# Half of two output projections taken forward, three weight loads issued before a gather, and one pair's weight slots refilled in halves

## The chip, the core and the metric

The kernel runs on one core of a Trainium2 chip. The metric is the time of the program on the device in microseconds (us). Five engines run their own instruction streams and meet only at semaphores: PE (TensorE, matrix products and transposes), DVE (VectorE), ACT (ScalarE), POOL (GpSimd) and SP (SyncE, which here only issues DMA transfers, in the order of its program). Weights come from the chip's main memory through 16 DMA engines that all queues of the core share.

## What is computed

One inference step of a one-layer hybrid encoder, in float32: 528 prompt rows (16 learned rows and 512) and 32 rows of a running stream, 1024 channels each. Only the parts near the change:

```
h = rmsnorm(x); proj = h @ w_in
a_out = silu(layernorm(causal_dwconv(glu(...))))            # 512 channels
b_out = head_rmsnorm(stick_breaking(q, k, v))               # 512 channels
x = x + concatenate([a_out, b_out]) @ w_out                 # (1024, 1024)
h2 = rmsnorm(x, g_ffn)
# routing: top-1 of 4 groups, then top-2 of 8 experts in it, weights p
for e in range(32):
    gu = h2 @ w_e_in[e]                                     # (1024, 512)
    out += gates[:, e] * ((silu(gu[:, :256]) * gu[:, 256:]) @ w_e_out[e])   # (256, 1024)
x = x + out; y = rmsnorm(x, g_final)
```

Every expert's weights are read: 2 MiB of w_e_in and 1 MiB of w_e_out each, 96 MiB in all.

## The kernel before

The rows are held in five chunks: four of 128 rows (chunks 0 to 3) and chunk 4 with 64 (16 prompt rows, 16 empty ones, 32 stream rows). The order of work on each engine is written out by hand.

**Output projection.** `project(c, ks, ns)` multiplies chunk c's mixed activations `mixt` with the eight row blocks k of `wout`. Blocks 4 to 7 belong to attention, 0 to 3 to the convolution; `LATE` is the order (4, 5, 6, 7, 0, 1, 2, 3). A product of 128 rows, one k and one half n of 512 columns is two matmul records in the trace. For chunks 0, 1 and 2 the attention half is done before the convolution's activations are ready, and `LATE[4:]` follows. Chunks 3 and 4 are projected whole, with all eight blocks. For chunk 4 the two halves n use the two column halves of the array. The results stand in PSUM banks `OUT_BANK` = (4, 2, 6, 2, 6), each with its neighbour.

**Around it**, per chunk: DVE's `residual(c)` adds the product to x (semaphore `x2_ready`), `normed_h2(c)` makes the normalized row block h2 (with a sum of squares on ACT and a root on POOL), SP stores it to `h2_dram`, PE's `turn_h2(c)` transposes it into banks 0 and 1, ACT copies it, PE's `logits(c)` multiplies it with the router's weights, and DVE's `choose(c)` and `place_at(c)` pick the two experts of each row and the row's place within the expert's tile; `positions(c)` on PE counts the rows ahead. PE's order is: project 0, project 1, turn 0, half of project 2, logits 0, turn 1, other half of project 2, logits 1, half of project 3, turn 2, positions 0, other half of project 3, positions 1, logits 2, project 4, turn 3, positions 2, logits 3, turn 4, logits 4, and then the tables. DVE's order is: residual and h2 of 0, 1, 2, then choose 0, choose 1, place 0, residual 3, place 1, h2 3, choose 2, residual 4, h2 4, place 2, choose 3, places, choose 4, places.

**Experts.** They run in 16 pairs. For pair g POOL gathers the rows of both experts (64 each) with an indirect DMA, PE transposes them (`turn`), multiplies with w_e_in (`gate_up`), ACT and DVE form the activation, PE transposes and multiplies with w_e_out (`down`), ACT scales, and POOL scatters to `y_dram`. w_e_in goes through seven slots `wi` (expert e in slot e % 7), w_e_out through seven slots `wo`. A slot's refill waits on SP for `gu_done` (gate_up of the pair) or `y_done` (down of the pair). Slot `wi[6]` lies over blocks 4 to 7 of `wout`; slot 4 over `mixt`; slot 5, in two pieces `wi5`, and `wo[4]` lie over the h2 buffers, the router's weights, its logits and the transposed h2.

Everything that SP issues stands in one program order, which around the change is: experts' loads 2, 3, 0, 1; stores of h2 0 to 3; expert 4; store of h2 4; expert 6; then, after the logits, the routing's subtraction (`gsub_ready`) and the landing of gather 0 (`gathered[0]`), slot 5, `wo[4]`; after `ent_ready` `wo[6]`; and then the refills pair by pair, experts 7 and 8 first.

Of the kernel before, what the change touches and what calls it, by code (L numbers as in the profile page):

```python
# [11 lines left out]
ALU = mybir.AluOpType  # L12
# [53 lines left out]
def build(nc, x_prompt, x_sample, cache_k, cache_v, cache_conv, meta, g_mix, w_in, conv_w, conv_b,  # L66
          ln_g, ln_b, g_sb, w_out, g_ffn, w_rg, b_rg, w_re, b_re, w_ei, w_eo, g_fin,
          y_p, y_s, nk_p, nv_p, ncv_p, nk_s, nv_s, ncv_s):
    with ExitStack() as ctx:
# [3 lines left out]
        def sem(name):  # L73
            return ctx.enter_context(nc.semaphore(name))
# [104 lines left out]
        wi5 = [(slice(0, 6), lowf[:, 9216:12288].rearrange("p (k n) -> p k n", k=6)),  # L179
               (slice(6, KD), lowf[:, 6144:7168].rearrange("p (k n) -> p k n", k=2))]  # L180

        def wi_at(e, k):

            if e % WI_SLOTS == 5:
                return wi5[k // 6][1][:, k % 6, :]
            return wi[e % WI_SLOTS][:, k, :]
# [102 lines left out]
        wi_end_loaded = wv_loaded[0:2]  # L289

# [156 lines left out]
        MEAN_BANK, LN_BANK = 2, 0  # L447
# [36 lines left out]
        def _(sp):  # L484
# [124 lines left out]
            sp.wait_ge(h2_stored[1], 16 * 2)  # L609
            sp.wait_ge(gsub_ready, 3)  # L610
# [264 lines left out]
        def _(pe):  # L875
# [268 lines left out]

            def project(c, ks, ns=(0, 1)):
                w = ROWS[c]

                def ready(k):
                    if k < NI and c == 0:
                        pe.wait_ge(mixa_ready, k + 1)  # L1150
                    elif k == NI:
                        pe.wait_ge(mixb_ready, mixed(c))

                if w < P:
                    for k in ks:
                        for n in ns:
                            mm = pe.matmul(ps[w * n:w * n + w, OUT_BANK[c] + n, :], mixt[:, k, P * c:P * c + w],
                                           wout[:, k, 512 * n:512 * n + 512], start=k == LATE[0], stop=k == LATE[-1],
                                           skip_group_check=True)
                    mm.then_inc(res_done, 1)  # L1160
                    return
                for n in ns:
                    for k in ks:
                        if n == ns[0]:
                            ready(k)
                        mm = pe.matmul(ps[0:w, OUT_BANK[c] + n, :], mixt[:, k, P * c:P * c + w],  # L1166
                                       wout[:, k, 512 * n:512 * n + 512], start=k == LATE[0], stop=k == LATE[-1],
                                       skip_group_check=True)
                if ks[-1] == LATE[-1] and ns[-1] == 1:
                    mm.then_inc(res_done, 1)  # L1170
# [117 lines left out]
            project(0, LATE[4:])  # L1288
            project(1, LATE[4:])
# [14 lines left out]
            project(4, LATE)  # L1304
# [27 lines left out]
            def gate_up(g):  # L1332
                for e in (2 * g, 2 * g + 1):
                    pe.wait_ge(wi_loaded[e % WI_SLOTS], (e // WI_SLOTS * 16 + 16) * (2 if e % WI_SLOTS == 5 else 1))
# [5 lines left out]
                for k in range(KD):  # L1340
# [399 lines left out]
        def _(dve):  # L1740
# [305 lines left out]
            def residual(c):  # L2046
# [3 lines left out]
                if w == P:  # L2050
                    dve.tensor_tensor(x[0:w, c, :].rearrange("p (a n) -> p a n", a=2), x[0:w, c, :].rearrange("p (a n) -> p a n", a=2),
                                      ps[0:w, OUT_BANK[c]:OUT_BANK[c] + 2, :], ALU.add).then_inc(x2_ready, 1)
                else:
                    for n in range(2):
# [3 lines left out]
            def normed_h2(c):  # L2058
# [25 lines left out]
                dve.tensor_scalar(h, h, stat[0:w, 32 + c:33 + c], None, ALU.mult).then_inc(h2_ready, 1)  # L2084

# [55 lines left out]
            normed_h2(0)  # L2141
            residual(1)
# [197 lines left out]
```

## Time and profile before

| | us |
|---|---|
| median of 3 runs | 561.22 |
| lowest and highest | 561.11, 561.43 |
| the profiled execution's own time | 562.51 |
| span of the profiled execution | 560.8 |
| PE busy | 507.7 (91%) |
| DVE busy | 267.4 (48%) |
| ACT busy | 165.8 (30%) |
| POOL busy | 146.3 (26%) |
| mean rate of all DMA over the span | 266 GB/s |

Times in the rows are counted from the start of the span. In a time line a row has start, duration, engine, line of the kernel, operation, output <- input with shapes, number of instructions, and in brackets how long the engine was idle before it and what ended that.

### The profile page before, as it was taken

How to read it: one execution, taken by the hardware profiler on the slowest of the kernel's cores; microseconds unless marked ns; L12 is line 12 of the kernel's file. 1: busy time of each engine (PE TensorE's matmuls, PEld its weight loads, DVE VectorE, ACT ScalarE, POOL GpSimd, SP SyncE). 2: the span in 40 equal slices, each digit the busy share in tenths (PEclk: the TensorE clock that was granted, in tenths of full speed). 3: DMA queues.
4: the chain of work that ended last, by engine and by line, in shares of the span. 5: the costliest groups of instructions: out<-in, count | busy, mean ns of one | idle time of the engine just before them, and what ended most of it. 6: DMA issues, size and time to landing. Idle time of an engine off the chain costs nothing.

```text
span 560.8 us, 7885 instructions
## 1 busy us (share of the span) xinstructions
PE 507.7 (91%) x3147; PEld 320.5 (57%) x3148; DVE 267.4 (48%) x471; ACT 165.8 (30%) x280; POOL 146.3 (26%) x143
## 2 busy tenths in 40 slices
PE   5999999999979889999997999999999678798993
PEld 5679999999847567545556634344434223333330
DVE  1870788999578897225668422111111111111157
ACT  4422555554476784032112011111111110111122
POOL 3002699998210102101021202111211110111003
PEclk9999999999979999999996899999999998999997
DMA  8902855500523602599117799999999999999994
GB/s 290 246 12 61 279 158 175 195 0 1 196 76 122 226 1 49 203 429 406 58 56 302 272 415 425 421 428 419 422 421 420 425 426 424 423 418 421 393 345 164
DMA packets 44763, 148.93 MB, mean 266 GB/s; under 512 B 7124, under 2 KB 23532, under 8 KB 36279
## 3 DMA queue, kind: packets, MB, share of 16 engines
q1 hardware_dynamic: 40263, 139.63, 64.3%
q0 software_dynamic: 4464, 8.80, 4.2%
q8 instruction: 25, 0.41, 0.3%
q14 instruction: 11, 0.09, 0.1%
HBM read 136.29 MB, written 19.59 MB: 278 GB/s over the span
## 4 chain that ended last, share of the span: by engine, by line
PE 61%; DMA 20%; DVE 9%; issue 4%; SPq 4%; ACT 1%; POOL 1%; DVEq 0%; POOLq 0%; ACTq 0%
PE ps L949 18%; DMA big<-in_w_expert_out 13%; PE ps L1166 10%; PE ps L1348 9%; PE ps L1373 5%; DMA cw<-h_dram,low 4%; PE ps L914 3%; DVE ps L1928 3%; SPq L628 2%; PE ps L1069 2%; PE ps L1329 2%; DMA y_dram<-cw,low 1%; PE ps L1017 1%; DMA big<-y_dram 1%; PE ps L902 1%
## 5 line engine op out<-in xcount | busy, mean ns | idle before, releaser
L2230 DVE TENSOR_TENSOR low<-low,ps 128x256 f32<-128x256 f32 x16 | 6.7, 422 | 173.2 <-ACT low L1700 173.2
L1348 PE MATMUL ps<-big,low 128*64 128x512 f32 x320 | 85.0, 593 | 3.7 <-issue 2.3
L949 PE MATMUL ps<-cw_r 128*128 128x280 f32 x256 | 72.3, 292 | 0.0
L949 PE MATMUL ps<-low_r,cw_r 128*128 128x280 f32 x256 | 72.2, 292 | 0.0
L949 PE MATMUL ps<-cw_r,big_r 128*128 128x280 f32 x256 | 72.1, 291 | 0.0
L1851 DVE SCALAR_TENSOR_TENSOR ps<-low,cwt,ps 128x590 f32<-128x590 f32 x80 | 66.9, 837 | 2.8
L1373 PE MATMUL ps<-big,low 128*64 128x512 f32 x160 | 46.9, 629 | 11.5 <-DMA big<-in_w_expert_out 4.6
L1166 PE MATMUL ps<-cw,low 128*128 128x512 f32 x128 | 56.6, 595 | 0.0
L1348 PEld LDWEIGHTS ps<-big,low 128*64 128x64 f32 x320 | 29.8, 137 | 46.0 <-issue 45.9
L734 POOL TENSOR_TENSOR big<-big 128x590 f32<-128x590 f32 x36 | 46.9, 1304 | 3.3
L949 PEld LDWEIGHTS ps<-cw_r 128*128 128x128 f32 x256 | 47.2, 188 | 0.4 <-issue 0.4
L949 PEld LDWEIGHTS ps<-cw_r,big_r 128*128 128x128 f32 x256 | 47.3, 188 | 0.0
L949 PEld LDWEIGHTS ps<-low_r,cw_r 128*128 128x128 f32 x256 | 47.2, 188 | 0.0
L1711 ACT ACTIVATE cw<-ps,low 128x1024 f32<-128x1024 f32 x16 | 17.8, 1115 | 98.1 <-PE ps L1373 98.1
L1348 PE MATMUL ps<-low 128*64 128x512 f32 x128 | 42.3, 593 | 0.2 <-issue 0.2
L814 POOL DMA_INDIRECT y_dram<-cw,low x15 | 15.1, 1009 | 101.7 <-ACT cw L1711 96.6
L802 POOL DMA_INDIRECT cw<-h_dram,low x16 | 16.6, 1035 | 94.1 <-PE ps L1329 82.5
L1166 PEld LDWEIGHTS ps<-cw,low 128*128 128x128 f32 x128 | 23.7, 190 | 26.8 <-issue 26.8
L1700 ACT ACTIVATE low<-ps 128x256 f32<-128x256 f32 x16 | 6.2, 384 | 108.5 <-PE ps L1348 108.5
L712 POOL TENSOR_TENSOR stat<-stat,nhalf 128x1 f32<-128x1 f32 (+2 forms) x16 | 15.3, 957 | 83.9 <-DVE stat L2075 32.6
L724 POOL TENSOR_TENSOR big_r<-big,cw_r 128x1024 fp32r<-128x1024 f32 x13 | 31.2, 2400 | 11.6 <-ACT cw_r L1494 11.6
L1373 PEld LDWEIGHTS ps<-big,low 128*64 128x64 f32 x160 | 14.8, 144 | 31.3 <-issue 31.3
(274 smaller groups left out, 816.7 us busy)
## 6 DMA issues: line engine op xcount, KB each, us to landing
big<-in_w_expert_in SPq DMA_DIRECT2D x16, 2048.0 KB, 20.6
big<-in_w_expert_out SPq DMA_DIRECT2D x20, 1024.0 KB, 26.1
big<-in_w_in SPq DMA_DIRECT2D x20, 512.0 KB, 5.3
low<-in_w_expert_out SPq DMA_DIRECT2D x8, 1024.0 KB, 31.5
low<-in_w_expert_in SPq DMA_DIRECT2D x4, 2048.0 KB, 23.3
cw<-in_w_expert_in SPq DMA_DIRECT2D x4, 2048.0 KB, 27.2
low<-in_w_expert_in SPq DMA_DIRECT2D x4, 1536.0 KB, 22.5
big<-in_w_expert_in SPq DMA_DIRECT2D x6, 1024.0 KB, 32.4
```

Source lines behind the costliest of these rows:

```text
L712: pool.tensor_tensor(t, t, nhalf[0:t.shape[0], :].broadcast_to(list(t.shape)), ALU.pow).then_inc(rstd_ready, 1)
L724: pool.tensor_tensor(w_lo[j % WSLOTS], win[j % WSLOTS], w_hi[j % HSLOTS].bitcast(F32), ALU.subtract).then_inc(w_lo_ready, 1)
L734: pool.tensor_tensor(conv[:, i, :], t, conv[:, i, :], ALU.add).then_inc(pool_tap_done, 1)
L802: pool.indirect_dma_start(out=xg_of(g), out_offset=None, in_=h2_dram, in_offset=bass.IndirectOffsetOnAxis(ap=rows_of[:, g, 0:1].bitcast(U3 ...
L914: mm = pe.matmul(ps[:, 4 + c % 2, :], h[:, k, cols], wts[:, k, :], start=m == 0 and k == 0, stop=m == 2 and k == KD - 1, skip_group_check= ...
L949: return pe.matmul(ps[:, proj_bank(j) + half, 0:PROJ], w[:, k, :], h[:, k, cols], start=first, stop=last, skip_group_check=True)
L1166: mm = pe.matmul(ps[0:w, OUT_BANK[c] + n, :], mixt[:, k, P * c:P * c + w], wout[:, k, 512 * n:512 * n + 512], start=k == LATE[0], stop=k = ...
L1348: mm = pe.matmul(ps[TILE * half:TILE * half + TILE, gu_bank(g), :], xt[:, k, TILE * half:TILE * half + TILE], wi_at(2 * g + half, k), star ...
L1373: mm = pe.matmul(ps[TILE * half:TILE * half + TILE, 4 + m, :], gact_t[:, k, TILE * half:TILE * half + TILE], wo[(2 * g + half) % WO_SLOTS] ...
L1711: act.activation((yg_end if g == PAIRS - 1 else yg[b]).rearrange("p (m n) -> p m n", m=2), ps[:, 4:6, :], ACT.Copy, scale=tab[:, g, 2:3]). ...
L1851: ins = dve.scalar_tensor_tensor(acc, src, w, acc, ALU.mult, ALU.add)
L1928: dve.tensor_tensor_scan(k, k, nones[:, 0:1].broadcast_to([P, n]), carry[:, a:a + 1] if cached else 1.0, ALU.mult, ALU.max).then_inc(left_ ...
```

## The change

Three things. (1) `project_late(3)` and `project_late(4)` do the attention half of chunks 3 and 4 right behind chunk 0's product, into banks 0/1 and 4/5, and DVE adds them to x with `residual_late`; the later calls do only the convolution's half. That leaves blocks 4 to 7 of `wout` unused from then on. (2) Expert 6's load, which lies over those blocks, is issued behind `project_late(4)`; slot 5 is cut in three pieces, of which two, and `wo[4]`, are issued after the logits and before gather 0 has landed. (3) Experts 7 and 8, which reuse the slots of pair 0, are loaded in halves: the first half once gate_up of pair 0 has done its first four blocks (`gu_half_done`), the second at `gu_done`.

```
-        wi5 = [(slice(0, 6), lowf[:, 9216:12288] ...),
+        wi5 = [(slice(0, 4), lowf[:, 9216:11264] ...),
+               (slice(4, 6), lowf[:, 11264:12288] ...),
                (slice(6, KD), lowf[:, 6144:7168] ...)]
+        LATE_BANK = {3: 0, 4: 4}
# SP
             load_one_wo(1)
+            sp.wait_ge(mean_done, 3)
+            load_wi(6)
             for c in range(NC):
...
-            load_wi(6)
             sp.wait_ge(logit_done, NC)
             sp.wait_ge(h2_stored[0], 16 * 3)
             sp.wait_ge(h2_stored[1], 16 * 2)
+            load_first_wi5(0)
+            load_first_wi5(2)
+            load_one_wo(4)
             sp.wait_ge(gsub_ready, 3)
             sp.wait_ge(gathered[0], 16)
-            load_wi(5)
-            load_one_wo(4)
+            load_first_wi5(1)
+            sp.wait_ge(gu_half_done, 1)
+            for e in (7, 8):
+                load_half(e, 0)
             sp.wait_ge(ent_ready, 1)
             load_one_wo(6)
             for g in range(RING, PAIRS - HALVED - 1):
-                load_wi(2 * g + 1)
-                load_wi(2 * g + 2)
+                if g == RING:
+                    sp.wait_ge(gu_done, 1)
+                    for e in (7, 8):
+                        load_half(e, 1)
+                else:
+                    load_wi(2 * g + 1)
+                    load_wi(2 * g + 2)
# PE
+            def project_late(c):
+                w = ROWS[c]
+                if c == 3:
+                    pe.wait_ge(co_ready, 2)
+                else:
+                    pe.wait_ge(x2_ready, 1)
+                for k in LATE[0:4]:
+                    for n in range(2):
+                        lo = w * n if w < P else 0
+                        mm = pe.matmul(ps[lo:lo + w, LATE_BANK[c] + n, :], mixt[:, k, P * c:P * c + w],
+                                       wout[:, k, 512 * n:512 * n + 512], ...)
+                mm.then_inc(mean_done, 1)
 turn_h2(0):
-                    pe.wait_ge(co_ready, 2)
+                    pe.wait_ge(dev_ready, NI + 1)
 logits(0):
+                    pe.wait_ge(dev_ready, NI + 3)
             project(0, LATE[4:])
+            project_late(3)
+            project_late(4)
             project(1, LATE[4:])
...
-            project(3, LATE, (0,))
+            project(3, LATE[4:], (0,))
...
-            project(3, LATE, (1,))
+            project(3, LATE[4:], (1,))
...
-            project(4, LATE)
+            project(4, LATE[4:])
 gate_up(g):
+                    if g == 0 and k == KD // 2 - 1:
+                        mm.then_inc(gu_half_done, 1)
# DVE
+            def residual_late(c):
+                w = ROWS[c]
+                dve.wait_ge(mean_done, c - 1)
+                if w == P:
+                    dve.tensor_tensor(halves(x[0:w, c, :]), halves(x[0:w, c, :]),
+                                      ps[0:w, LATE_BANK[c]:LATE_BANK[c] + 2, :], ALU.add).then_inc(dev_ready, 1)
+                    return
+                for n in range(2):
+                    ...                                   # one add for each half of 512 columns
             normed_h2(0)
+            residual_late(3)
+            residual_late(4)
             residual(1)
```

residual(3) and residual(4) wait for `dev_ready` too, and gate_up of the pairs with experts 7 and 8 for `wi_half_loaded`.

## Rows read from the trace of the kernel before

**Rows 1.** The page: rate of all DMA in 40 slices of 14 us; the software queue
```profile
GB/s 290 246 12 61 279 158 175 195 0 1 196 76 122 226 1 49 203 429 406 58 56 302 272 415 425 421 428 419 422 421 420 425 426 424 423 418 421 393 345 164
...
q0 software_dynamic: 4464, 8.80, 4.2%
```

**Rows 2.** The chain of waits: start us, us, what
```profile
243.08 13.73 PE ps L1166 x32
...
285.52 7.04 PE ps L1157 x32
...
327.71 6.87 PE ps L1348 x32
...
418.62 37.62 DMA big<-in_w_expert_out
```

**Rows 3.** Time line of PE: logits of chunk 4, gate_up of pair 0
```profile
298.90 1.89 PE L1232 MATMUL ps<-low 128*64 128x36 f32 x16 [0.30 <-ACT low L1663]
...
314.88 7.09 PE L1348 MATMUL ps<-big,low 128*64 128x512 f32 x32
```

**Rows 4.** Time line of DVE, residual(2) to residual(4)
```profile
267.21 1.22 DVE L2051 TENSOR_TENSOR x<-x,ps 128x1024 f32<-128x1024 f32 x1 [5.58 <-PE ps L1166]
...
272.05 0.19 DVE L2091 TENSOR_TENSOR low<-ps,bias 128x36 f32<-128x36 f32 x1
...
274.57 0.19 DVE L2091 TENSOR_TENSOR low<-ps,bias 128x36 f32<-128x36 f32 x1
...
277.75 0.19 DVE L2114 TENSOR_REDUCE low<-low 128x1 f32<-128x32 f32 x1
283.78 1.22 DVE L2051 TENSOR_TENSOR x<-x,ps 128x1024 f32<-128x1024 f32 x1 [5.85 <-PE ps L1166]
...
291.68 0.19 DVE L2104 TENSOR_TENSOR low<-negs 128x32 bf16<-128x32 f32 x1
292.58 1.40 DVE L2056 TENSOR_TENSOR x<-x,ps 64x512 f32<-64x512 f32 x2 [0.71 <-PE ps L1157]
```

**Rows 5.** Stretches: length, busy time by engine, granted clock of PE, DMA share, GB/s
```profile
268.00:293.00 25.00, 25.00 (x104) 12.35 (x104) 15.90 (x55) 3.31 (x5) 3.04 (x3) 1.00 0.11 43
293.00:294.00 1.00, 1.00 (x13) 0.99 (x11) 0.95 (x2) 0.70 (x2) 1.00 (x1) 1.00 0.92 180
293.00:306.00 13.00, 9.27 (x100) 8.41 (x99) 11.36 (x46) 2.99 (x7) 2.74 (x2) 0.71 0.91 340
312.00:323.00 11.00, 11.00 (x94) 6.19 (x93) 5.38 (x21) 0.39 (x1) 0.99 (x1) 0.99 0.92 338
418.00:520.00 102.00, 83.92 (x392) 34.43 (x390) 14.35 (x22) 9.38 (x13) 13.81 (x14) 0.97 1.01 422
480.00:500.00 20.00, 17.21 (x77) 6.85 (x74) 1.98 (x3) 1.50 (x2) 3.03 (x3) 0.91 1.02 422
```

**Rows 6.** Time line of SP's issues
```profile
292.58 0.34 SPq L576 DMA_DIRECT2D low<-in_w_expert_in  x1
...
298.41 0.59 SPq L576 DMA_DIRECT2D cw<-in_w_expert_in  x1
311.88 0.80 SPq L574 DMA_DIRECT2D low<-in_w_expert_in  x2
312.72 0.43 SPq L581 DMA_DIRECT2D low<-in_w_expert_out  x1
319.29 0.33 SPq L581 DMA_DIRECT2D cw<-in_w_expert_out  x1
322.00 0.80 SPq L576 DMA_DIRECT2D big<-in_w_expert_in  x2
...
334.61 0.81 SPq L576 DMA_DIRECT2D big<-in_w_expert_in  x2
```

**Rows 7.** Time line of POOL: the issue of gather 0
```profile
308.29 1.30 POOL L802 DMA_INDIRECT cw<-h_dram,low  x1 [11.32 <-DVE low L2177]
```

**Rows 8.** All gathers (line 802): from issue to landing
```profile
DMA to landing us min/median/max: 3.4/10.0/11.3
```

More of the change, by code:

```diff
@@ L178, in build @@
               for t in [slots[q][:, 0:4096] for q in (2, 3, 0, 1, 4, 5)] + [cw[:, 4096:8192]]]
-        wi5 = [(slice(0, 6), lowf[:, 9216:12288].rearrange("p (k n) -> p k n", k=6)),
+        wi5 = [(slice(0, 4), lowf[:, 9216:11264].rearrange("p (k n) -> p k n", k=4)),
+               (slice(4, 6), lowf[:, 11264:12288].rearrange("p (k n) -> p k n", k=2)),
                (slice(6, KD), lowf[:, 6144:7168].rearrange("p (k n) -> p k n", k=2))]
@@ L184, in wi_at @@
             if e % WI_SLOTS == 5:
-                return wi5[k // 6][1][:, k % 6, :]
+                ks, t = wi5[(0, 0, 0, 0, 1, 1, 2, 2)[k]]
+                return t[:, k - ks.start, :]
             return wi[e % WI_SLOTS][:, k, :]
@@ L289, in build @@
         wi_end_loaded = wv_loaded[0:2]
+        wi_half_loaded = sem("wi_half_loaded")
+        gu_half_done = sem("gu_half_done")
         const_ready = sem("const_ready")
@@ L446, in build @@
         OUT_BANK = (4, 2, 6, 2, 6)
-        MEAN_BANK, LN_BANK = 2, 0
+        MEAN_BANK, LN_BANK, LATE_BANK = 2, 0, {3: 0, 4: 4}
         acc = ps[:, 6:8, :].rearrange("p b n -> p (b n)")[:, 0:CW]
@@ L609, in _, with load_first_wi5, load_half @@
             sp.wait_ge(h2_stored[1], 16 * 2)
+            def load_first_wi5(n):
+                ks, dst = wi5[n]
+                sp.dma_start(dst, w_ei[0, 5].rearrange("(p k) n -> p k n", p=P)[:, ks]).then_inc(wi_loaded[5], 16)
+            load_first_wi5(0)
+            load_first_wi5(2)
+            load_one_wo(4)
             sp.wait_ge(gsub_ready, 3)
             sp.wait_ge(gathered[0], 16)
-            load_wi(5)
-            load_one_wo(4)
+            load_first_wi5(1)
+            def load_half(e, half):
+                ks = slice(4 * half, 4 * half + 4)
+                sp.dma_start(wi[e % WI_SLOTS][:, ks], w_ei[0, e].rearrange("(p k) n -> p k n", p=P)[:, ks]).then_inc(
+                    wi_loaded[e % WI_SLOTS] if half else wi_half_loaded, 16)
+            sp.wait_ge(gu_half_done, 1)
+            for e in (7, 8):
+                load_half(e, 0)
             sp.wait_ge(ent_ready, 1)
@@ L1143, in _ @@
             LATE = (4, 5, 6, 7, 0, 1, 2, 3)
+            def project_late(c):
[7 more added lines that the diff above has]
+                        lo = w * n if w < P else 0
+                        mm = pe.matmul(ps[lo:lo + w, LATE_BANK[c] + n, :], mixt[:, k, P * c:P * c + w], wout[:, k, 512 * n:512 * n + 512],
+                                       start=k == LATE[0], stop=k == LATE[3], skip_group_check=True)
+                mm.then_inc(mean_done, 1)
             def project(c, ks, ns=(0, 1)):
-                w = ROWS[c]
+                w, first = ROWS[c], LATE[0 if c < 3 else 4]
                 def ready(k):
@@ L1157, in project @@
                             mm = pe.matmul(ps[w * n:w * n + w, OUT_BANK[c] + n, :], mixt[:, k, P * c:P * c + w],
-                                           wout[:, k, 512 * n:512 * n + 512], start=k == LATE[0], stop=k == LATE[-1],
+                                           wout[:, k, 512 * n:512 * n + 512], start=k == first, stop=k == LATE[-1],
                                            skip_group_check=True)
@@ L1166, in project @@
                         mm = pe.matmul(ps[0:w, OUT_BANK[c] + n, :], mixt[:, k, P * c:P * c + w],
-                                       wout[:, k, 512 * n:512 * n + 512], start=k == LATE[0], stop=k == LATE[-1],
+                                       wout[:, k, 512 * n:512 * n + 512], start=k == first, stop=k == LATE[-1],
                                        skip_group_check=True)
@@ L1333, in gate_up @@
                 for e in (2 * g, 2 * g + 1):
-                    pe.wait_ge(wi_loaded[e % WI_SLOTS], (e // WI_SLOTS * 16 + 16) * (2 if e % WI_SLOTS == 5 else 1))
+                    pe.wait_ge(wi_loaded[e % WI_SLOTS], (e // WI_SLOTS * 16 + 16) * (len(wi5) if e % WI_SLOTS == 5 else 1))
+                if 7 in (2 * g, 2 * g + 1) or 8 in (2 * g, 2 * g + 1):
+                    pe.wait_ge(wi_half_loaded, 32)
                 pe.wait_ge(xt_ready, g + 1)
@@ L2050, in residual @@
                 if w == P:
+                    if c == 3:
+                        dve.wait_ge(dev_ready, NI + 1)
                     dve.tensor_tensor(x[0:w, c, :].rearrange("p (a n) -> p a n", a=2), x[0:w, c, :].rearrange("p (a n) -> p a n", a=2),
@@ L2053, in residual @@
                 else:
+                    dve.wait_ge(dev_ready, NI + 3)
                     for n in range(2):
@@ L2084, in normed_h2 @@
                 dve.tensor_scalar(h, h, stat[0:w, 32 + c:33 + c], None, ALU.mult).then_inc(h2_ready, 1)
+            def residual_late(c):
+                w = ROWS[c]
+                dve.wait_ge(mean_done, c - 1)
+                if w == P:
+                    dve.tensor_tensor(halves(x[0:w, c, :]), halves(x[0:w, c, :]), ps[0:w, LATE_BANK[c]:LATE_BANK[c] + 2, :],
+                                      ALU.add).then_inc(dev_ready, 1)
+                    return
+                for n in range(2):
+                    cols = slice(512 * n, 512 * n + 512)
+                    dve.tensor_tensor(x[0:w, c, cols], x[0:w, c, cols], ps[w * n:w * n + w, LATE_BANK[c] + n, :],
+                                      ALU.add).then_inc(dev_ready, 1)
             def choose(c):
```

## The prediction

> **What bounds the kernel now.** I read the slices of the page first, then the chain of waits, then the time lines around the edit. In the slices [rows 1] the reader is to see two regimes: up to about 290 us the DMA engines have whole slices of nothing, and from about 315 us they move 415 to 428 GB/s without a break until slice 38. The stretches say the same [rows 5]: share 1.01 at 422 GB/s from 418 us to 520 us. In the chain [rows 2] PE sets the pace up to 292.6 us, and at 418.62 it goes over to weights that land 38 us after their issue. Between 323 and 418 us PE follows its own pace, about 12.6 us a pair (the gate-and-up products of pairs 0 and 1 start at 314.88 [rows 3] and 327.71 [rows 2]). A pair brings 6 MiB, 6.29 MB, which are 14.9 us at 422 GB/s. So the queue grows from pair to pair and never empties; PE's early slack is used up at about 418 us. The end is the moment at which DMA became continuously busy, plus the bytes left then, divided by 422 GB/s. A change counts here by how it moves that moment or those bytes, not by how early PE starts.
>
> **Where the bytes stand before.** From 312 to 323 us the engines moved 338 GB/s, 3.72 MB [rows 5]. What was issued from 311.88 us on and had to pass before experts 7 and 8 is the rest of slot 5, 2.10 MB, w_out of experts 4 and 6, 2.10 MB [rows 6], and two gathers at 8.80 MB / 31 = 0.28 MB each [rows 1]: 4.76 MB. 1.04 MB were left at 323, 2.5 us. So the bytes that start with expert 7's weights, call them R, begin at 325.4 us although they were issued at 322.0. The queue had them waiting.
>
> **The change, part by part.**
> *The late blocks in front of chunk 1.* Chunk 3's attention half is 8 products, 6.9 us: the row at 243.08 [rows 2] holds 16 such products (32 records, a product is two) in 13.73 us. Chunk 4's is half of the 7.04 us at 285.52 [rows 2], 3.5 us. Together 10.4 us, none of it new work: the same products leave the later calls. But PE has no idle time here (the chain of [rows 2] is PE's own from 243.08, and 25.00 of the 25 us from 268 to 293 are busy, [rows 5]), so all that follows chunk 0's product moves back by 10.4 us: chunk 1 to 260.4 to 267.2, turn_h2(0), chunk 2 and logits(1) to 279.3. residual(2), at 267.21 before [rows 4], comes at 277.6.
> *What is given back.* From residual(2) on, VectorE carries the chain. Its row at 283.78 waited 5.85 us and the one at 292.58 waited 0.71 us [rows 4]. The shortened products of chunk 3 (3.4 us less in each half) and chunk 4 can give back no more than these waits. In numbers, by the spacing of [rows 4]: residual(2) at 277.6, h2 of chunk 2 at 282.5 (4.84 us on), choose(0) done 285.0 (2.5 us on), which releases positions(0) and with it the second half of chunk 3, four products, at 285.1 to 288.55; meanwhile choose(1) and place_at(0) end at 288.35 (5.9 us from the start of choose(0)). So residual(3) starts at 288.65, 4.9 us later than before. place_at(1), normed_h2(3) and choose(2) take the 8.1 us that they took before (283.78 to 291.87), and end at 296.75; chunk 4's product has been done since 294.0, so residual(4) starts there, against 292.58: 4.2 us late. Behind it the chain is the old one (root, turn_h2(4), logits(4), choose(4), the places), without spare waits but the small ones that it has. Delay of the table, the gathers and all of PE's expert work: D = 4.2 us.
> *The three new adds on VectorE* cost what L2051 costs, 1.22 us, and L2056's pair, 1.40 us [rows 4]. They run at 257 to 262 us, where VectorE now waits for chunk 1: nothing. Uncovered they would be 2.6 us. The new waits on dev_ready are met by 258 and 262, before PE comes to turn_h2(0) at 267.3 and logits(0) at 271.5. The wait on mean_done in SP's queue holds the store of h2 chunk 0 from 258.6 to 260.8; nobody needs that buffer before 279.
> *Expert 6's weights* (2.10 MB, 5 us) go out at 260.4 instead of 298.41 [rows 6] and land in the empty stretch behind 268 us [rows 5]. Nothing waits for it. *Two parts of slot 5 and w_out of expert 4* (2.62 MB, 6.2 us) go out when logits(4) is done, 298.90 + 1.89 + 4.2 = 305.0 [rows 3], and drain by about 312.4 (6.2 us at 422 GB/s, and 1.1 us to the first bytes, below). Gather(0), 308.29 + 4.2 = 312.5 [rows 7], lands 3.4 us behind its issue [rows 8] and moves its 0.28 MB in the last of these, so it just misses them. The last part of slot 5 follows the gather at 316.1.
> *The halves.* Gate-and-up of pair 0 starts at 314.88 + 4.2 = 319.05 and gives back its first halves after 3.55 us (half of 7.09, [rows 3]), at 322.6. Experts 7 and 8's first halves start to flow some 1.1 us later, 323.7: expert 4's load, issued at 292.58 [rows 6], has the engines 0.92 busy from 293 to 294 us [rows 5]. The second halves follow at 326.1, with no gap, since first halves and expert 6's w_out (issued now at 323.5) make 3.15 MB, 7.5 us.
> *The sum.* In the new order 1.05 MB of w_out (2.5 us) stand beside R. R's equivalent start is 323.7 + 2.5 = 326.2. Up to the next release, gu_done of pair 1 (the issue at 334.61, [rows 6]) + 4.2 = 338.8 (flowing at 339.8), the queue holds 6.58 MB with a scatter and expert 7's w_out: it drains at 323.7 + 15.6 = 339.3, so a gap of 0.5 us opens that did not exist. From there on the queue grows as before. 326.7 - 325.4 = +1.3, with a little for ramps +1.4 us. In general the shift is D - 2.8 us: the early loads and halves are worth 2.8 us, the late blocks' place costs 4.2.
>
> The profiled execution took 562.51 us with a span of 560.8; the median of the runs is 561.22, close to the span. I add 1.4 to both: span 562.2, time 562.6.
>
> *What the trace does not show, with bounds.* The time from issue to flow after a wait: 0.4 us (one issue's own length, [rows 6]) to 3.4 us (a whole gather to its landing, [rows 8]), taken 1.1 as at expert 4, which is the same kind of issue; a gather is another kind, so little weight goes to that end. The gap at 339 us: 0 to 1.2 us. D: 3.6 us, if choose(0) comes through faster than counted, to 4.9, the delay at residual(3). Together the likeliest case's own range is +0.1 to +2.8 us. Halved loads could move less per second; the closest row says no: between 480 and 500 us only loads of 1 MiB or less are in the queue (load_part and load_wo of the last pairs), and the stretch moves 422 GB/s [rows 5]. The Trainium skill, "DMA: Bandwidth & Descriptors", section "Bandwidth", gives 341 GB/s for a single transfer of 1 MB; by that the four halves would cost 2.4 us more, and the row beside it disagrees because they queue behind each other.
>
> **The rivals.**
> *The late blocks cost nothing, faster.* If all 10.4 us came back in the shorter calls, D would be 0 and the shift -2.8 us: 558.4. It decides from D below 2.8 us downwards, in VectorE's rows between residual(2) and residual(4). For it: VectorE waited 5.58 + 5.85 + 0.71 us in that region [rows 4]. Against it: the 5.58 lie ahead of residual(2), where PE itself is 10.4 us behind. 10 in 100.
> *PE's clock falls earlier.* PE now has waits of 1.3 us at 283.7, 1.7 us at 295 and 1.5 at 298, where it had none before 295. Before, the granted clock fell from 1.00 to 0.50 (2.4 to 1.2 GHz) at about 299 us, after PE had been busy 9.3 of 13 us [rows 5]. Should it fall at 285, half of chunk 3 costs 3.4 us more, chunk 4's product 3.5 us, of which 0.7 reaches VectorE: D = 8.3, shift +5.5, 566.7. Against it: in the stretch from 284 to 294 PE would be busy about nine tenths. That waits drop the clock is also what the Trainium skill says, "TensorE: Matmul & The Clock Gate", section "HAM oscillation"; the trace agrees at 299 us. 10 in 100.
> *The early loads hit gather(0).* If 2.62 MB drain later than 312.3, the gather's packets share the engines with them. Uncovered it lands in 3.4 us, among loads in 10.0 us at the median [rows 8]; only a tail of 1 to 2 us could overlap here. D and so the shift grow by as much: 564.0. 10 in 100.
> *The queue moves halves more slowly*, the 2.4 us above: 565.0. 3 in 100.
> *As worked out*, 562.6: 67 in 100.
>
> **How the numbers follow.** A measurement of this kernel tells about 0.2%, 1.1 us, from no change. Of the likeliest case (+0.1 to +2.8) some 6 parts in 10 lie over +1.1 us and the rest within; the clock, the collision and the slow halves are slower nearly throughout; the free late blocks are faster in most of their width. Faster 0.13, same 0.30, slower 0.57. The range: the likeliest case's own is 561.3 to 564.0; with a part of the rivals on both sides 560.2 to 565.2.
>
> **What the profile after would show.** residual(3) waits well under 1 us for PE and starts near 288.7; residual(4) does not wait at all and starts near 296.8; gather(0) near 312.5, gate-and-up of pair 0 near 319.0; expert 6's load at 260.4, in a stretch that was empty; DMA nearly idle from 313 to 323 except for gathers and half a megabyte; continuous from 323.7 on. The last pairs wait for w_out as before, each about 1.4 us later. The prediction is wrong if D is not 4.2 us, if the queue was not continuously busy in one of the two kernels (then PE's delay or its absence counts in full), or if the empty stretch behind the gather turns out shorter.

## The result, and the profile after

| | before | after |
|---|---|---|
| median, us | 561.33 (561.11 to 561.55, 4 runs) | 565.64 (564.93 to 566.76, 4 runs) |
| span of the profiled execution, us | 560.8 | 565.0 |

The changed kernel is slower by 4.3 us: ratio 1.0079, 95% interval 1.0061 to 1.0096. The forecast was 562.6 us with a range of 560.2 to 565.2: the sign was right, the size was three times too small, and the time lies 0.4 us above the range. Both profiled executions were slower than the medians, by about the same: the one before took 562.51 us (1.2 above), the one after 566.76 (1.1 above, the slowest of its four).

DVE's time line after, in the stretch that answers to [rows 4]:

```profile
277.60 1.22 DVE L2099 TENSOR_TENSOR x<-x,ps 128x1024 f32<-128x1024 f32 x1 [5.41 <-PE ps L1205]
...
284.97 0.18 DVE L2153 TENSOR_TENSOR low<-ps,bias 128x36 f32<-128x36 f32 x1
285.83 0.23 DVE L2157 TENSOR_SCALAR low<-low 128x4 f32<-128x4 f32 x1
...
288.92 1.22 DVE L2099 TENSOR_TENSOR x<-x,ps 128x1024 f32<-128x1024 f32 x1 [0.59 <-PE ps L1205]
...
295.27 0.99 DVE L2157 TENSOR_SCALAR low<-low 128x4 f32<-128x4 f32 x1
...
297.68 1.39 DVE L2105 TENSOR_TENSOR x<-x,ps 64x512 f32<-64x512 f32 x2
...
304.57 0.20 DVE L2153 TENSOR_TENSOR low<-ps,bias 128x36 f32<-128x36 f32 x1 [1.11 <-PE ps L1272]
```

residual(2) stands at 277.60 as forecast, residual(3) at 288.92 with a wait of 0.59 us (forecast 288.65, "well under 1 us"). Then the account slips twice. residual(4) is at 297.68, not 296.75: L2157, a tiny operation of 0.23 us, took 0.99 us. It is part of choose(2), and it ran beside POOL's memset of `cw`, which is shown below. And choose(3), the row at 304.57, waits 1.11 us for PE, where before the change it waited for nothing.

Before the change the same operation and the memset (DVE and POOL) were apart:

```profile
290.14 0.23 DVE L2095 TENSOR_SCALAR low<-low 128x4 f32<-128x4 f32 x1
292.61 1.81 POOL L790 MEMSET cw<- 128x2048 f32 x1 [4.11 <-PE ps L1157]
```

PE in the same stretch, and POOL's memset and gather 0:

```profile
297.90 2.61 PE L1325 MATMUL ps<-ident 128*128 128x128 f32 x12
300.87 3.60 PE L1272 MATMUL ps<-low 128*128 128x36 f32 x16 [0.35 <-ACT low L1707]
...
321.26 7.09 PE L1392 MATMUL ps<-big,low 128*64 128x512 f32 x32
```

```profile
294.33 1.91 POOL L815 MEMSET cw<- 128x2048 f32 x1 [0.70 <-PE ps L1196]
300.76 1.34 POOL L737 TENSOR_TENSOR stat<-stat,nhalf 64x1 f32<-64x1 f32 x1 [4.53 <-DVE stat L2128]
314.48 1.30 POOL L827 DMA_INDIRECT cw<-h_dram,low  x1 [12.39 <-DVE low L2241]
```

logits(3), the second row of PE, takes 3.60 us for 16 records, in place of 1.95 before the change (1.95 or 1.96 in every trace of the old order, and the duration of logits(2) in this one). Before:

```profile
295.78 1.95 PE L1232 MATMUL ps<-low 128*128 128x36 f32 x16 [0.72 <-ACT low L1661]
```

The stretches say why: PE's granted clock is 0.50 (1.2 GHz) from 300 us on. In single microseconds it is 1.00 (2.4 GHz) up to 298 us, 0.62 from 298 to 299 and 0.50 from 299, after PE had been busy 0.8 of the 3 us from 295 to 298.

```profile
294.00:300.00 6.00, 3.53 (x24) 3.05 (x23) 5.49 (x16) 1.62 (x5) 1.91 (x1) 0.85 0.81 295
300.00:306.00 6.00, 5.52 (x31) 5.02 (x31) 4.04 (x14) 1.47 (x3) 1.34 (x1) 0.50 0.53 186
312.00:324.00 12.00, 11.87 (x110) 9.79 (x109) 7.38 (x37) 1.83 (x4) 3.32 (x3) 0.72 0.67 224
324.00:326.00 2.00, 2.00 (x12) 0.72 (x9) 1.43 (x7) 0.00 (x0) 0.00 (x0) 1.00 0.15 33
326.00:328.00 2.00, 2.00 (x12) 0.69 (x8) 0.00 (x0) 0.00 (x0) 0.00 (x0) 1.00 0.87 266
328.00:345.00 17.00, 15.56 (x80) 7.06 (x80) 3.96 (x6) 1.88 (x3) 2.06 (x2) 1.00 1.01 410
```

The last columns are the granted clock, the DMA share and GB/s. Gather 0 is issued 6.19 us later than in [rows 7], gate_up of pair 0 starts 6.38 us later than in [rows 3]. From 312 to 316 us the early loads still flow (DMA share 0.96), from 316 to 326 us DMA is busy for less than half of the time (0.45, 127 GB/s); in [rows 5] 312 to 323 us were 0.92 busy. SP's issues, against [rows 6]:

```profile
260.19 0.33 SPq L580 DMA_DIRECT2D cw<-in_w_expert_in  x1
...
307.56 0.82 SPq L618 DMA_DIRECT2D low<-in_w_expert_in  x2
308.42 0.43 SPq L585 DMA_DIRECT2D low<-in_w_expert_out  x1
318.49 0.33 SPq L618 DMA_DIRECT2D low<-in_w_expert_in  x1
324.94 0.80 SPq L628 DMA_DIRECT2D big<-in_w_expert_in  x2
325.79 0.43 SPq L585 DMA_DIRECT2D cw<-in_w_expert_out  x1
328.38 0.80 SPq L628 DMA_DIRECT2D big<-in_w_expert_in  x2
```

Everything went out early as intended, and the queue had run dry by 324 us (0 GB/s from 324 to 325). It is the row at 324.94 that starts the continuous stretch. The chain of waits ends as before, only later: its last wait for w_out and the product behind it are, before and after,

```profile
484.95 33.32 DMA big<-in_w_expert_out
518.47 3.67 PE ps L1373 x16
...
489.73 32.99 DMA big<-in_w_expert_out
522.81 3.67 PE ps L1419 x16
```

The product is 4.3 us later, the whole of the difference.

### The profile page after: what moved, and what is told of

It is laid out like the page before. It is cut to its first block, busy times and chain, and to the rows that moved or that the text cites. A ratio compares the mean times of both kernels' runs of the same rounds, so it can differ in the third digit from the quotient of the medians.

```text
span 565.0 us, 7896 instructions
## 1 busy us (share of the span) xinstructions
PE 508.4 (90%) x3147; PEld 322.3 (57%) x3148; DVE 270.7 (48%) x474; ACT 165.9 (29%) x280; POOL 147.5 (26%) x143
## 4 chain that ended last, share of the span: by engine, by line
PE 58%; DMA 20%; DVE 9%; SPq 6%; issue 3%; ACT 2%; POOL 1%; DVEq 0%; POOLq 0%; ACTq 0%
PE ps L974 18%; DMA big<-in_w_expert_out 12%; PE ps L1205 8%; PE ps L1392 7%; PE ps L1419 5%; DMA cw<-h_dram,low 4%; PE ps L939 3%; DVE ps L1974 3%; DMA big<-y_dram 2%; SPq L653 2%; PE ps L1180 2%; SPq L585 2%; PE ps L1094 2%; PE ps L1371 2%; DMA y_dram<-cw,low 1%
## 5 line engine op out<-in xcount | busy, mean ns | idle before, releaser
L1392 PE MATMUL ps<-big,low 128*64 128x512 f32 x320 | 85.0, 593 | 5.1 <-issue 3.9
L1392 PEld LDWEIGHTS ps<-big,low 128*64 128x64 f32 x320 | 29.8, 137 | 47.4 <-issue 47.4
L1419 PE MATMUL ps<-big,low 128*64 128x512 f32 x160 | 43.8, 597 | 11.6 <-DMA big<-in_w_expert_out 4.7
L1205 PE MATMUL ps<-cw,low 128*128 128x512 f32 x112 | 50.0, 596 | 0.0
L1205 PEld LDWEIGHTS ps<-cw,low 128*128 128x128 f32 x112 | 20.6, 190 | 23.3 <-issue 23.3
L1974 DVE TENSOR_TENSOR_SCAN ps<-ps,negs 128x128 f32<-128x128 f32 (+4 forms) x36 | 26.2, 753 | 11.9 <-ACT ps L1639 10.1
```

The source lines that it names most:

```text
L1419: mm = pe.matmul(ps[TILE * half:TILE * half + TILE, 4 + m, :], gact_t[:, k, TILE * half:TILE * half + TILE], wo[(2 * g + half) % WO_SLOTS] ...
L1974: dve.tensor_tensor_scan(k, k, nones[:, 0:1].broadcast_to([P, n]), carry[:, a:a + 1] if cached else 1.0, ALU.mult, ALU.max).then_inc(left_ ...
```

## The experiments

Medians stand beside those of the kernel before on the same chip (561.86 for e1 to e4, 561.91 for e5 to e8, 561.73 for e9 to e12, 562.00 for e13 to e16). These differ by up to 0.7 us from the 561.33 beside which the changed kernel's 565.64 stands, so kernels of different groups are compared by their distance from the kernel before in their own group. For the changed kernel that distance is +4.3 us, and +3.8 us in its second measurement (e9). "First half issued" is the issue that answers to 324.94 above.

### The two parts of the change by themselves

**e1**: late blocks and expert 6's early load alone (the edit is against the changed kernel, as in e2).

```
-            load_first_wi5(0)
-            load_first_wi5(2)
-            load_one_wo(4)
             sp.wait_ge(gsub_ready, 3)
             sp.wait_ge(gathered[0], 16)
+            load_first_wi5(0)
             load_first_wi5(1)
+            load_first_wi5(2)
+            load_one_wo(4)
-            sp.wait_ge(gu_half_done, 1); load_half(7, 0); load_half(8, 0)
...
-            sp.wait_ge(gu_done, 1); load_half(7, 1); load_half(8, 1)
+            load_wi(7); load_wi(8)
```

> The changed kernel with the late blocks in front of chunk 1 and expert 6's early load kept, but slot 5 and w_out of expert 4 issued behind gather(0) as before, and experts 7 and 8 loaded whole at gu_done. Delay theory (the place of the late blocks holds the experts' start back by D = 6.4 us, the early loads and halves give some 2 to 3 us back): gather(0) stays near 314.5 us, DMA gets nothing back, so the whole D reaches the end: 561.3 + 6.3 = 567.6 us. Rival (the split and early loads cost the time, the late blocks are harmless): 561 to 563 us.

567.14 us, ratio 1.0092 (1.0075 to 1.0109): +5.3 us, about as expected. The late blocks with expert 6's early load cost more than the whole change; the rival falls. The trace of this kernel also shows one thing that the later experiments need: here logits(3) ran at full clock.

```profile
300.88 1.95 PE L1268 MATMUL ps<-low 128*128 128x36 f32 x16 [1.38 <-ACT low L1699]
```

and gather 0 was issued at 313.37, 1.1 us earlier than in the changed kernel's trace, with the same order of work up to there.

**e2**: the loads alone, the projections as before.

```
-            project_late(3)
-            project_late(4)
-            project(3, LATE[4:], (0,)) ... project(3, LATE[4:], (1,)) ... project(4, LATE[4:])
+            project(3, LATE, (0,)) ... project(3, LATE, (1,)) ... project(4, LATE)
-            sp.wait_ge(mean_done, 3)
-            load_wi(6)                   # back behind the store of h2 4
```

> The changed kernel with the projections of chunks 3 and 4 whole and in their old places, expert 6's load in its old place; slot 5 and w_out of expert 4 still early, experts 7 and 8 still in halves. Delay theory: VectorE and PE run as before the change, but 2.62 MB are issued near 301 us behind expert 6's 2.1 MB, so that gather(0), issued at 308.3, meets them: it lands 1 to 3 us later than 311.9. That is D = 1 to 3 us against about 2.1 us given back: 560.2 to 562.2 us. Rival (the split and early loads cost the time): 564 us or more.

566.61 us, 1.0077 (1.0060 to 1.0094): +4.8. A miss for the delay theory as I had put a number on it. The rival's number (564 us or more) came out, but not for its reason: e5 has the split loads and the halves and is faster than the kernel before. The price of the collision was not 1 to 3 us. The profiled execution is a slow one: it took 569.90 us, the other four 565.56 to 566.70. Its chain of waits:

```profile
308.23 7.82 DMA cw<-h_dram,low
316.09 1.97 PE ps L1367 x8
318.06 2.40 PE ps L1315 x40
320.46 9.64 PE ps L1388 x32
```

Gather 0 took 7.8 us instead of 3.5. In the ten us before its issue 4.7 MB of weights had been issued (expert 6's, slot 5's pieces and w_out), and part of them was still in front of it: up to its landing DMA moved 278 GB/s, 2.2 MB, of which two gathers are 0.56, which leaves some 1.6 MB of weights. PE had nothing to do from 312.5 us on and its granted clock fell to 0.50. The transposes, the gate table and the first part of gate_up ran at that clock: 1.97, 2.40 and 9.64 us against 0.87, 1.41 and 7.09. The first half was issued at 326.71, later than in the changed kernel.

**e4**: all loads, PE's order kept (the PE part of the edit is shown against the kernel before). Attention's half of chunk 3 stands where its first column half stood, and nothing is moved ahead of chunk 2.

```
-            project(3, LATE, (0,))
+            project(3, LATE[0:4])
             turn_h2(2)
             positions(0)
-            project(3, LATE, (1,))
+            project(3, LATE[4:])
...
-            project(4, LATE)
+            project(4, LATE[0:4])            # then_inc(mean_done)
+            project(4, LATE[4:])
# SP, in front of expert 4's load
+                    sp.wait_ge(mean_done, 2)
+                    load_wi(6)
```

> All loads of the change, but with PE's work in an order that keeps chunk 2's place: attention's half of chunk 3 (both column halves) goes where its first column half stood, the convolution's half where its second stood, chunk 4 likewise in two halves at its old place; expert 6's load is issued behind chunk 4's attention half (about 289 us); no extra adds on VectorE. Delay theory: D = 0, slot 5 and w_out of expert 4 go out near 302 us and drain before gather(0): the early loads and halves give their 2 to 2.8 us: 558.5 to 559.3 us. Rival (what the early loads give is nothing): 561.3 us.

564.88 us over ten runs from 561.6 to 567.1, 1.0055 (1.0035 to 1.0074): +3.0 us, again a miss, and above the rival too. So with the late blocks back in their place all the early loads together still make the kernel slower. The delay of the late blocks is gone (gather 0 is issued at 307.86), but slot 5 and w_out went out only at 303.3, since SP waited 5.2 us for the store of h2 4, issued behind 4.2 MB of loads, and they met the gather (profiled execution, 563.12 us):

```profile
307.86 6.27 DMA cw<-h_dram,low
314.18 1.09 PE ps L1369 x8
315.27 1.62 PE ps L1316 x40
316.89 8.38 PE ps L1390 x32
```

Up to the landing DMA moved 297 GB/s, 1.9 MB, so some 1.3 MB of weights were in front of gather 0.

**e5**: e4 with 1 MiB less: w_out of expert 4 goes behind gather 0.

```
             load_first_wi5(0)
             load_first_wi5(2)
-            load_one_wo(4)
             sp.wait_ge(gsub_ready, 3)
             sp.wait_ge(gathered[0], 16)
             load_first_wi5(1)
+            load_one_wo(4)
```

> The kernel with the old order of PE's work (chunks 3 and 4 in halves at their old places, expert 6's load behind chunk 4's attention half), and of the early loads only slot 5's two pieces (1.57 MB); w_out of expert 4 goes behind gather(0). They are issued near 303.3 us, as slot 5 and w_out were, and drain by 308.1, so gather(0), issued at 308, meets nothing and lands within 3.4 to 3.7 us; PE's spare matmuls reach up to it and the clock stays up. Delay theory: 2 to 3 us faster than before, 559 to 560 us, and steadier than with all three early. Rival (the halves and an empty queue cost as much as they give, whatever gather(0) does): 561.5 us or more.

559.85 us over ten runs (559.1 to 561.4), 0.9966 (0.9954 to 0.9978): 2.1 us faster than the kernel before, and 5.0 us faster than e4. In its trace gather 0 lands 3.5 us after its issue, gate_up of pair 0 starts at 314.91, as in [rows 3] (D = 0), and the span is 558.0 against 560.8. That is just the 2.8 us which the prediction gave to the early loads and halves, with some luck: the traced execution of the kernel before was a slow one (562.51), this one lies at its median. The medians say 2.1.

```profile
314.91 7.09 PE L1390 MATMUL ps<-big,low 128*64 128x512 f32 x32
```

**e6**: e4 with slot 5 and w_out both behind gather 0.

> As the last, but slot 5 and w_out of expert 4 behind gather(0) as before the change; only expert 6's load is early and experts 7 and 8 come in halves. Gather(0) lands at 311.5 as before, DMA is then busy without a break up to and beyond the halves, which only change their order with w_out of expert 6. Delay theory: no byte starts earlier than before, 561.3 to 561.9 us, as steady as before. Rival (halved loads cost by themselves): 563 us or more.

561.07 us, 0.9984 (0.9972 to 0.9995): 0.8 us faster, a little more than expected. Why it is faster at all is open: the old queue moved 344 GB/s in the microsecond behind 322 us, and 430 GB/s flow from 322 to 324 us here, but over one microsecond that is worth only 0.2 us. The halves do not cost by themselves.

**e15 and e16**: whole loads at gu_done in the changed kernel and in e5 (the last hunk of e1).

> The changed kernel with experts 7 and 8 loaded whole at gu_done of pair 0. By the account of the queue their first bytes flow 3.4 us later, but expert 6's w_out goes first and fills 2.5 us of it: +0.4 to +1 us, 566.0 to 566.6 us. Rival (halved loads cost more than they give): 565.6 us or less.

> The faster version (e5) with experts 7 and 8 loaded whole at gu_done. By the account of the queue +0.4 to +1 us, 560.2 to 560.9 us. Rival (the halves are what made e5 faster than before): 561.7 us.

566.41 us, 1.0080 (1.0063 to 1.0097), and 561.04 us, 0.9985 (0.9975 to 0.9994). Both times lie in or just above their ranges. In e5 the halves are worth 1.1 us (-2.1 us with them, -1.0 without). In the changed kernel the distance from the kernel before is +4.4 us without them and +4.3 or +3.8 with them, so a gain there, 0.1 to 0.6 us, is not clear of noise. Of e5's 2.1 us the early pieces of slot 5 (with expert 6's load) give some 1.0.

**e11**: the edit that made e5 of e4, made in the changed kernel.

> The changed kernel with w_out of expert 4 behind gather(0): the one edit that took 5 us off e4. Here gather(0) is issued at 314.5 and the three loads are out by 315.8, so it lands 0.4 us earlier at best and the w_out load still fits the empty stretch before the halves. Delay theory: 565.2 to 565.6 us, no change beyond 0.5 us. Rival (early w_out of expert 4 costs by itself, wherever gather(0) is): 561 to 562 us.

566.73 us, 1.0090 (1.0073 to 1.0106): 1.2 us slower than the changed kernel on the same chip (e9), so the edit helps only where gather 0 is in the way. That it costs more than 0.5 us here was not expected (the two intervals overlap a little); in the trace DMA has 315 GB/s from 320 to 324 us against 170 in e9, but the bytes moved by 330 us agree within 0.1 MB, so I do not know where the rest is lost.

### How a delay of PE passes to the end

**e7 and e8**: 24 in place of 12 spare matmuls in front of turn(0), in the kernel before and in the changed one.

```
-            busy(WARM)
+            busy(2 * WARM)
```

> The kernel before, with 24 spare matmuls in place of 12 in front of turn(0): nothing but a delay of PE by some 2.6 us between gather(0) and the first transposes. Cushion theory (before the change, the refills of pair 0's slots queue for 3.4 us behind slot 5 and w_out loads, so PE may be late by that much; after it the queue is empty and each us of PE's passes to the end): no more than +0.5 us, 561.9 to 562.4 us. Rival (the end follows PE's start in both kernels): +2.6 us, 564.5 us.

> The changed kernel with the same 12 further spare matmuls in front of turn(0), some 2.6 us. Cushion theory: DMA is idle when the first halves are issued, so the delay passes in full: 565.6 + 2.6 = 568.2 us. Rival (the queue takes it up, as it does PE's own variation): 565.6 to 566.1 us.

564.28 us, 1.0045 (1.0025 to 1.0064), and 569.22 us, 1.0130 (1.0103 to 1.0157). In the traces PE is late by 2.4 and 2.8 us at gate_up, and the span is 1.4 and 2.5 us longer; the medians rose by 2.4 us, and by 3.0 or 3.5 us (+7.3 against +4.3 or +3.8). The changed kernel passes everything on, as expected. For the kernel before this is a miss: at most 0.5 us was expected, and it passed on all of the 2.4. A reason that fits is in its issues: w_out of expert 6 waits for `ent_ready`, which hangs on the same transposes, and it went out at 321.63 in place of 319.29, so the queue ran low from the other end (254 GB/s from 322 to 323 us).

**e13 and e14** put 12 spare matmuls behind the gate table, where they delay gate_up but not `ent_ready`.

```
             turn(0)
             gate_table()
+            busy(12)
```

> The kernel before with 12 spare matmuls (2.6 us) between the gate table and gate_up of pair 0, behind everything on which expert 6's w_out load waits. Queue theory (3.4 us of the refills' wait are queue, not PE): no more than +0.5 us, 561.7 to 562.3 us. Rival (PE's delay passes on in any case): +2.6 us, 564.3 us.

> The changed kernel with the same 12 spare matmuls in the same place. Queue theory: DMA is idle when the first halves are released, but expert 6's w_out is not delayed and fills 2.5 us of the wait, so some of the delay is hidden: +0.5 to +2.6 us, 566.1 to 568.2 us, and more than in e13. Rival (no difference between the two kernels): the same increase as e13.

563.62 us, 1.0033 (1.0021 to 1.0046), and 569.12 us, 1.0132 (1.0115 to 1.0149): +1.6 us, and +2.8 or +3.3 us (+7.1 against +4.3 or +3.8). Both are misses: at most +0.5 and +2.6 were expected. That e14 rises more than e13 was expected and holds. In the profiled execution of e13 gate_up starts at 316.85, 2.0 us late, and the span is 560.7, the same as before the change; but that execution (562.52 us) is the fastest of its eight, and the one before was slower than its median. Its DMA moved 229 GB/s from 324 to 327 us, behind the issue of expert 7's load at 323.98; against 422 GB/s that is 1.4 us lost. So before the change the queue hides at most about 1 us of PE's delay, after it none. A cushion of 3.4 us, as my account of the bytes had it, is not there.

### PE's clock

**e3 and e12** fill PE's new waits.

```
             turn_h2(2)
+            pe.wait_ge(x2_ready, 3)
+            busy(5, 7)                       # five spare matmuls into bank 7
             positions(0)
...
             turn_h2(3)
-            positions(2)
             pe.wait_ge(x2_ready, 4)
-            busy(6)
+            busy(7)
+            positions(2)
+            busy(10)
```

> The changed kernel with more spare matmuls where PE waits: 5 in front of positions(0), 7 in front of positions(2), 10 in place of 6 behind it. They compute nothing that is used. Clock theory (1.1 us of the delay comes from logits(3) running at 1.2 GHz for 3.60 us in place of 1.95, since PE idled before it): granted clock 1.0 at logits(3), choose(3) no longer waits 1.1 us for it, gather(0) 1 us earlier, total 565.6 - 1.1 = 564.5 us. Rival (PE's early delay is taken up by the DMA queue and the clock does not matter for the end): 565.6 us with gather(0) 1 us earlier.

> The kernel of e3 (more spare matmuls around positions(0) and positions(2)) once more, beside the changed kernel on the same chip. Clock theory: 1.0 to 1.5 us below the changed kernel's median beside it. Rival: the same time within 0.5 us, because the clock then falls elsewhere on the way to gate-and-up of pair 0.

Both traces show what was to be shown (the rows are e12's):

```profile
300.76 1.95 PE L1272 MATMUL ps<-low 128*128 128x36 f32 x16 [0.49 <-ACT low L1710]
...
319.55 7.09 PE L1395 MATMUL ps<-big,low 128*64 128x512 f32 x32
```

logits(3) at full clock, gate_up 1.6 and 1.7 us earlier, and spans of 562.9 in both against 565.0 and 564.4 (the changed kernel and e9). But the medians are 565.79 and 565.63 us, +3.9 us in both, against +4.3 and +3.8. The traced executions are not typical: those of e3 and e12 are the fastest of their four, those of the changed kernel and of e9 the slowest. The clock theory holds in the traced executions and is not seen over all of them; in the medians both rivals have it right.

**e9**: the changed kernel once more.

> The changed kernel once more, for a second trace and more times. If the granted clock at logits(3) is set anew in each execution, this trace may show 1.95 us there in place of 3.60, and then gather(0) near 313.4 and a span near 563; if it is fixed by the order of the work, 3.60 us again, gather(0) at 314.5 and a span of 565. Times 565 to 567 us in either case.

565.51 us, 1.0062 (1.0046 to 1.0079); logits(3) 3.60 us again, span 564.4. Over the seven traces with the changed kernel's order of work and no spare matmuls there, it is 3.60 us in four (the changed kernel, e8, e9, e11) and 1.95 us in three (e1, e14, e15). Up to that point e14 runs the same instructions as the changed kernel. So the clock at that point differs from execution to execution, and holding it can be worth only part of what the traces show. Both ways were seen in traces only; how often each happens is not known.

**e10**: e4 with 20 spare matmuls in front of turn(0).

```
-            busy(WARM)
+            busy(WARM + 8)
```

> The kernel of e4 (old order of PE's work, all three early loads), with 20 spare matmuls in place of 12 in front of turn(0), so that PE has work until the delayed gather(0) lands. Collision and clock theory (e4 loses 2.4 us to the gather's later landing and on average 2 to 3 us more to PE's clock falling while it waits for it): clock 1.0 through gate-and-up of pair 0, 7.09 us, and 562 to 563 us, steadier than e4's 561.6 to 567.1. Rival (the collision costs all of it, the clock nothing): 564.9 us or, with the spare matmuls in the way, more.

563.72 us over eight runs, 1.0037 (1.0016 to 1.0058): +2.0 us against e4's +3.0, above the 562 to 563 expected, and the two intervals overlap. In its trace gate_up runs at full clock, 7.09 us, from 316.88. Keeping the clock up may win back about 1 us, which is not clear of noise; the executions still scatter from 561.7 to 566.8, so what makes e4 unsteady is not the clock in gate_up alone.

## Why the prediction was right in sign and wrong in size

*That the late blocks are not hidden* held to 0.3 us as far as residual(3): 288.92 against 288.65. e1 shows the cost of their place (+5.3 us, with expert 6's early load), and e5, with PE's order kept and the same loads but for one, w_out of expert 4 behind gather 0, is 2.1 us faster than the kernel before. In the changed kernel it is the place of `project_late` that costs the time. But that is not the only way to slower: with all the loads and PE's order kept (e4) the kernel is 3.0 us slower as well, by the collision with gather 0, which the late blocks' delay had kept away.

*The step that failed* is the term D = 4.2 us, in two sentences: that place_at(1), normed_h2(3) and choose(2) "take the 8.1 us that they took before", and that behind residual(4) "the chain is the old one ..., without spare waits but the small ones that it has". residual(4) was 5.1 us late in place of 4.2, and 1.1 us more came behind it: D was 6.2 us at the gather and 6.4 at gate_up, beyond the 3.6 to 4.9 given for it. Two things lengthened the chain that I had counted as unchanged:

- DVE's L2157, 0.98 or 0.99 us in place of 0.23 in all nine traces with this order of work (the changed kernel, e1, e3, e8, e9, e11, e12, e14, e15), each time under POOL's memset of `cw`, and never in a trace where the memset falls elsewhere. Before the change the memset ran beside residual(4), 292.61 against 292.58, whose duration was the same 1.40 us as without it. L2157 stands in choose(2), in front of residual(4): +0.8 us, as much as the vanished wait of 0.7 us had given back.
- logits(3) at half clock in the traced execution, 3.60 us in place of 1.95, of which 1.1 reach DVE as a wait. It differs from execution to execution: in e1, e14 and e15 it did not happen, and gather 0 went out 5.1 to 5.4 us late. The clock was a rival of mine, but with its price taken at the wrong place: I had it fall at 285 us under chunk 3's and 4's products (566.7 us). It fell between 298 and 299 us, as before the change, only that logits(3) was now behind that point. (The "9.3 of 13 us" in that rival is a misreading: that stretch, 293 to 306 us, lies mostly behind the fall. From 295 to 298 us, just before it, PE was busy 2.1 of 3 us before the change.)

*The pay-back of 2.8 us* is 2.1 us by e5's median, where D is 0; that e5's span is shorter by exactly 2.8 is partly luck. Its premise, that pair 0's refills stood 3.4 us in a full queue before, is not borne out (e7, e13). With D = 6.4 the formula gives +3.6 us, and the trace shows +4.2. Part of the remainder is the term "time from issue to flow", taken as 1.1 us: the halves were issued at 324.94, and from 326 to 328 us only 266 GB/s moved. What is missing there against 422 GB/s is 0.31 MB, 0.7 us.

*Gather 0 among the early loads* happened only mildly in the changed kernel (issue to landing 3.9 us in place of 3.5), though the loads, issued at 307.56 in place of 305.0, drained only at about 316; D had carried the gather away from the loads. So that rival had hardly a part in this result. In e2 and e4, where D is 0, it is the main cost, and the 1 to 3 us that I had given it in e2 were too little: 2.8 to 4.3 us of waiting and then PE's clock on top. One MiB decides there between 564.9 and 559.9 us.

*That halves are moved more slowly*, by 2.4 us, is excluded: with them e5 is 1.1 us faster (e16), and the changed kernel not slower (e15). The 341 GB/s for a single transfer of 1 MB in the Trainium skill ("DMA: Bandwidth & Descriptors", section "Bandwidth") do not apply to a queue of such loads; it moved 410 GB/s from 328 to 345 us here. The row that the prediction had set against it was read too widely: a load of 2 MiB, issued at 455.61, landed only at 495 us, so not all loads between 480 and 500 us were of 1 MiB or less. From 500 to 520 us, behind it, the rate was 420 GB/s.

*Open*: why the executions of e4 and e10 scatter by 5.5 and 5.1 us where ten of e5 stay within 2.3 and twenty of the kernel before within 2.2 (the changed kernel's four lie within 1.8); what e11 and e6 lose and gain; how often the clock falls early; and how large the cushion of the old queue is.

## What to carry to other kernels

Work that frees a buffer early is not free because its sum is unchanged: count how much of what it pushes back is given back, and that is no more than the waits that the next engine had behind that point. When an early load is moved into an idle stretch, look at what small transfer on the critical path starts at its end; cut the load until it drains before that (here one MiB less turned +3.0 us into -2.1). And a chain of short operations that is moved in time is to be recounted against what now runs beside it on the neighbouring engines, the clock of TensorE included.

## What the runs showed of the hardware that was not expected

A VectorE tensor_scalar on 128x4 elements took 0.98 to 0.99 us in place of 0.23 when it began during a GpSimd memset of 128x2048 (1.90 to 1.92 us), in all nine traces with the late blocks in front of chunk 1; the operations ahead of it in that chain, a tensor_tensor with one input in PSUM, a scalar_tensor_tensor and two reduces, kept their durations beside the same memset (0.19, 0.22 and 0.16 us). In the trace of the changed kernel the memset ends at 296.24 and the tensor_scalar at 296.26, and in all nine the two ends are within 0.03 us, so it looks like one that stood still until the memset was done. The Trainium skill has the rule ("SBUF — State Buffer", section "SBUF: two separate sides"): a VectorE operation in a mode that uses two ports, and a GpSimd operation, exclude one another, whoever starts first holds the shared ports to its end, while a VectorE operation with two inputs in SBUF is held only by a GpSimd operation that reads SBUF.
A gather of 0.28 MB landed 6.3 us after its issue with some 1.3 MB of weights still in front of it (e4) and 7.8 us after it with some 1.6 MB (e2), against 3.5 us with almost nothing in front (e5, and the kernel before). The bytes are estimates, from what DMA moved up to the landing less two gathers. At 422 GB/s 1.3 and 1.6 MB are 3.1 and 3.8 us, so the gather waited about as long as what stood in front of it took.
